# Gate and up projections of two SwiGLU layers by seven block products instead of eight, with the gated products spilled to DRAM and the down projection as a phase of its own

## The chip, the core and the metric

The kernel runs on one core of a Trainium2 chip. The metric is the device time of one execution in microseconds, as the median of several runs. TensorE multiplies, VectorE and ScalarE evict its results from PSUM and do the elementwise work, GpSimd works from SBUF alone, and DMAs are issued from the queues of SyncE and ScalarE.

## The reference

Two residual layers over 1024 tokens of width 1024, all in float32. Each layer is a mixer followed by a SwiGLU feed-forward of width 2816, and each of the two halves is normalised and modulated first:

```python
h = rms_norm(x, norm_ffn_g[l]) * (1 + sc2) + sh2
x = x + g2 * swiglu(h, ffn_w_gate[l], ffn_w_up[l], ffn_w_down[l])

def swiglu(h, w_gate, w_up, w_down):
    return (jax.nn.silu(h @ w_gate) * (h @ w_up)) @ w_down
```

The six modulation vectors of a layer come from a product of the conditioning vector with `ada_w[l]` (1024 x 6144). The mixer of layer 0 is a gated convolution beside a retention, that of layer 1 is a stick-breaking attention. The change touches only the feed-forward and the work at its edges.

## The kernel before

Activations lie transposed: `xT` and the normalised input `h` are [128 features, 8 feature tiles, 1024 tokens], and each is worked on in two halves of 512 tokens, h = 0 and 1. Every float32 product is made of three fp32r products: both operands are split into a high part and the rest, and `three` issues high x high, high x low and low x high, each a matmul of 128 x 128 weights with 128 x 512 moving data. One projection of 128 outputs for one half is 8 feature tiles x 3 = 24 matmuls into one of the four PSUM banks of `psG`.

The program is a list of phases in a fixed order, and every engine's queue is written out by hand with semaphores. Around the change the phases are out0 (output projection of the mixer), norm1, ffn0, norm2, qkv0 in layer 0 and out1, norm3, ffn1 and the writing of the output in layer 1.

A feed-forward phase (`ffn0`, `ffn1`) is eleven turns. A turn takes 256 hidden features: four weight slabs (gate and up for two tiles of 128) and two slabs of the down weight. SyncE loads a slab (512 KB) into one of two raw buffers, and GpSimd splits it in four quarters into an 8 KB slot: four TENSOR_SCALAR for the high part, then four TENSOR_TENSOR for the rest. TensorE makes 8 gate and up projections (192 matmuls). ScalarE applies SiLU from PSUM, VectorE multiplies (`L1959`) and splits the product (`L1553`, `L1555`) into `hid`. Then TensorE makes the 16 down steps of the turn, 6 matmuls each, and VectorE adds every step to `xT` (`L1975`). Nothing of the hidden layer leaves the core.

Beside ffn0 the modulation of layer 1 is worked out: SyncE loads pieces of `ada_w` (`ada_raw`, two buffers, four pieces in a turn), VectorE accumulates them (`L1567`, two operations a piece), and one small group of matmuls per turn (`ada_group`) brings the sums into columns.

norm1 and norm3 follow an output projection: ScalarE squares `xT`, VectorE adds the squares, a matmul with ones takes the mean, ScalarE takes the root (Ln, Exp), VectorE refines it (`newton`, four operations), and then each tile is normalised (`L1629`), rounded by ScalarE (`norm_hi`) and its rest taken by VectorE (`L1620`). Half 0 is normalised beside the projection of half 1. Half 1 is normalised beside the first four projections of half 0 in the feed-forward, 96 matmuls.

## Time and profile before

| | us |
|---|---|
| median of 3 runs | 2635.77 |
| lowest and highest run | 2628.8 and 2636.09 |
| span of the profiled execution | 2618.4 |
| median less span | 17.4 |
| TensorE busy | 2532.1 (97%) |
| GpSimd busy | 976.8 (37%) |
| ffn0, first to last matmul of the down steps | 563.3 to 1249.9 |
| ffn1, the same | 1929.5 to 2607.5 |

No time of its own is listed for the profiled execution, only its span, from the first to the last instruction. What lies around the span is taken as median less span. A matmul's duration in the trace overlaps the next one, so the pace of TensorE is read from a stretch with a count of matmuls, not from the duration of one.

### The profile page before, as it was taken

What the parts mean: (1) busy time and instruction counts of PE and PEld (TensorE: products, weight loads), DVE (VectorE), ACT (ScalarE), POOL (GpSimd) and SP (SyncE); (2) the same over time, 40 slices, a digit from 0 to 9 for tenths busy, and PEclk for the clock granted to TensorE, in tenths of its full rate; (3) what the DMA queues carried; (4) which work ended last, traced back from release to release, by engine and by line L of the source; (5) the groups of instructions that cost most, each with busy time, mean ns of one, the idle gap of its engine ahead of it and who ended that gap; (6) DMA issues with size and microseconds to landing.
All of it is one profiled execution on the core that took longest, in us unless ns stands there. A gap on an engine that the chain in (4) does not pass through costs nothing.

```text
span 2618.4 us, 34125 instructions
## 1 busy us (share of the span) xinstructions
PE 2532.1 (97%) x11386; PEld 2077.7 (79%) x11386; DVE 1317.7 (50%) x2082; ACT 562.8 (21%) x1031; POOL 976.8 (37%) x1604
## 2 busy tenths in 40 slices
...
GB/s 277 174 129 97 137 125 276 50 81 81 80 80 80 80 80 80 80 72 49 89 21 45 33 33 32 45 57 140 49 49 48 48 48 48 48 48 48 48 32 65
DMA packets 220646, 208.31 MB, mean 80 GB/s; under 512 B 6122, under 2 KB 166020, under 8 KB 220420
## 3 DMA queue, kind: packets, MB, share of 16 engines
...
## 4 chain that ended last, share of the span: by engine, by line
PE 89%; DVE 6%; issue 2%; ACT 2%; DMA 1%; ACTq 0%; POOL 0%; DVEq 0%; SPq 0%; POOLq 0%
PE psG L632 27%; PE psG L638 26%; PE psG L637 26%; PE psM L983 1%; PE psG L1024 1%; PE psO L632 1%; PE psZ L1013 1%; PE psO L637 1%; PE psO L638 1%; DVE n_t L1629 1%; DVE h_lo L1620 1%; PE psZ L632 1%; PE psZ L638 1%; PE psZ L637 1%; PE psM L683 0%
## 5 line engine op out<-in xcount | busy, mean ns | idle before, releaser
L632 PE MATMUL psG<-h_hi,w_split 128*128 128x512 f32 x2496 | 990.7, 397 | 26.1 <-DVE h_lo L1555 13.4
L637 PE MATMUL psG<-h_lo,w_split 128*128 128x512 f32 x2496 | 976.7, 391 | 0.0
L638 PE MATMUL psG<-h_hi,w_split 128*128 128x512 f32 x2496 | 976.4, 391 | 0.0
L611 POOL TENSOR_SCALAR w_split<-w_raw 128x256 fp32r<-128x256 f32 x800 | 362.5, 480 | 1566.6 <-PE psG L632 514.2
L615 POOL TENSOR_TENSOR w_split<-w_raw,w_split 128x256 fp32r<-128x256 f32 x800 | 622.8, 810 | 0.0
L632 PEld LDWEIGHTS psG<-h_hi,w_split 128*128 128x128 f32 x2496 | 471.6, 189 | 132.6 <-issue 19.8
L638 PEld LDWEIGHTS psG<-h_hi,w_split 128*128 128x128 f32 x2496 | 471.1, 189 | 100.8
L637 PEld LDWEIGHTS psG<-h_lo,w_split 128*128 128x128 f32 x2496 | 471.9, 189 | 98.7 <-issue 4.1
L1959 DVE TENSOR_TENSOR hid<-sil,psG 128x512 f32<-128x512 f32 x88 | 60.6, 688 | 721.2 <-PE psG L638 718.6
L1975 DVE SCALAR_TENSOR_TENSOR xT<-psG,mod,xT 128x512 f32<-128x512 f32 x352 | 259.6, 748 | 168.5 <-PE psG L638 168.3
L1125 ACT ACTIVATE sil<-psG 128x512 f32<-128x512 f32 x88 | 52.5, 599 | 1293.4 <-PE psG L638 1293.3
L632 PE MATMUL psG<-hid_hi,w_split 128*128 128x512 f32 x704 | 274.8, 390 | 0.8 <-DVE xT L1975 0.8
L638 PE MATMUL psG<-hid_hi,w_split 128*128 128x512 f32 x704 | 274.0, 389 | 0.0
L637 PE MATMUL psG<-hid_lo,w_split 128*128 128x512 f32 x704 | 273.9, 389 | 0.0
L632 PEld LDWEIGHTS psG<-hid_hi,w_split 128*128 128x128 f32 x704 | 132.1, 188 | 29.7 <-issue 2.3
L638 PEld LDWEIGHTS psG<-hid_hi,w_split 128*128 128x128 f32 x704 | 132.1, 188 | 27.6
L637 PEld LDWEIGHTS psG<-hid_lo,w_split 128*128 128x128 f32 x704 | 132.2, 188 | 27.1
L1567 DVE SCALAR_TENSOR_TENSOR ada_acc<-ada_raw,c_act,ada_acc 128x512 f32<-128x512 f32 x140 | 115.6, 825 | 7.5 <-DMA ada_raw<-in_ada_w 4.5
L1125 ACT ACTIVATE s_z<-s_z 128x128 f32<-128x128 f32 (+2 forms) x192 | 100.9, 525 | 6.1
L1555 DVE TENSOR_TENSOR hid_lo<-hid,hid_hi 128x512 fp32r<-128x512 f32 x88 | 69.3, 788 | 3.0
L1555 DVE TENSOR_TENSOR s_w<-s_w,s_w 128x128 fp32r<-128x128 f32 (+2 forms) x96 | 63.9, 665 | 3.3
L1125 ACT ACTIVATE n_sq<-xT 128x512 f32<-128x512 f32 x48 | 30.0, 630 | 140.3 <-DVE n_sum L1597 56.3
...
## 6 DMA issues: line engine op xcount, KB each, us to landing
ada_raw<-in_ada_w SPq DMA_DIRECT2D x80, 512.0 KB, 4.1
w_raw<-in_ffn_w_gate SPq DMA_DIRECT2D x44, 512.0 KB, 3.9
w_raw<-in_ffn_w_up SPq DMA_DIRECT2D x44, 512.0 KB, 3.8
w_raw<-in_ffn_w_down SPq DMA_DIRECT2D x44, 512.0 KB, 3.7
w_raw<-in_ev_w_in SPq DMA_DIRECT2D x28, 512.0 KB, 4.6
w_raw<-in_od_w_qkv SPq DMA_DIRECT2D x24, 512.0 KB, 3.9
...
x_spill<-xT ACTq DMA_DIRECT2D x2, 4096.0 KB, 12.6
```

The source lines that it names most:

```text
L611: nc.gpsimd.tensor_scalar(slot[:, 0, part], raw[:, part], 1.0, 1.0, ALU.mult, ALU.mult).then_inc(hi_done, 1)
L615: lo = nc.gpsimd.tensor_tensor(slot[:, 1, part], raw[:, part], slot[:, 0, part].bitcast(F32), ALU.subtract)
L632: mm = nc.tensor.matmul(o, st[0], mv[0], start=first, stop=False, **kw)
L637: nc.tensor.matmul(o, st[0], mv[1], start=False, stop=False, **kw)
L638: return nc.tensor.matmul(o, st[1], mv[0], start=False, stop=end, **kw)
L983: misc(phase, i, 2 * off + e, [lambda: nc.tensor.matmul(psM[:], ones_head, s_sq[:], start=True, stop=True)])
L1013: mm = nc.tensor.matmul(zbank[t % ZRING][:, c0:], split_c[:, 1], s_s[:, t % SRING, n, c0:], start=False, stop=n == 1, skip_group_check=True)
L1125: return nc.scalar.activation(o, i_, f, **kw)
L1555: V.tensor_tensor(o[1], i_, o[0].bitcast(F32), ALU.subtract).then_inc(lo_sem, 1)
L1567: V.scalar_tensor_tensor(acc, src, cc, acc, ALU.mult, ALU.add).then_inc(ada_step, 1)
L1959: V.tensor_tensor(hid32[:], sil[f][:], psG[:, bank(phase, s)], ALU.mult).then_inc(bank_read[bank(phase, s)], 1)
L1975: V.scalar_tensor_tensor(xT[:, m, half(h)], psG[:, b], mod[:, l * MOD + 5 * KT + m:l * MOD + 5 * KT + m + 1], xT[:, m, half(h)], ALU.mult, ...
```

## The change

For each pair i of 128-feature tiles (256 hidden features, as a turn before) the product of a weight matrix (gate or up) with the input is cut in 2 x 2 blocks: two hidden tiles by two halves of the feature dimension (k 0 to 3 and 4 to 7), and two halves of the tokens. It is made by seven block products (Winograd's form of Strassen's product) of 4 feature tiles x 3 = 12 matmuls, for gate (m = 0) and up (m = 1): 14 products, 168 matmuls.

- The sums of input blocks (`t1` to `t4`) are made once a layer, after the norm, by VectorE, rounded by ScalarE, and their rests are taken by VectorE or GpSimd (`t_sum`, `t_low`). The normalised tiles are written in place into `xT`, so `xT` is first written to DRAM by halves (`x_spill`, waited for through `fx_out`).
- The sums of weight blocks (`w_sum`, 8 a pair) are made by GpSimd for each pair, from raw slabs in four buffers `f_raw`. ScalarE makes the high part of a weight block (`w_high`), GpSimd its rest (`f_block`), into a ring of 8 blocks `f_w`. For the first 8 blocks of a layer GpSimd makes both.
- The four outputs are put together from PSUM and three stored sums by VectorE (`first_y`, `second_y`, `out_12`, `out_21`), then SiLU, product, rounding and rest, and the split product goes to DRAM (`f_spill`, 4 x 512 KB a pair).
- The down projection follows as a phase of its own (`ffb0`, `ffb1`), six turns over 1, 2, 2, 2, 2 and 2 pairs, 16 steps each: 6 matmuls a step in turn 0, 12 in the others. The split products are loaded back (`hid_load`, 2 MB a pair), for turn j + 1 as turn j begins. `x_old` is loaded from DRAM for turn 0.
- The 40 pieces of `ada_w` are loaded and accumulated in turns 1 to 4 of ffb0, and their loads are issued by ScalarE.
- The loops over turns are written out.

The layout of `h`, some slots and the order in which norm2's tiles are normalised change with it.

```diff
-CHUNKS = D_FF // P // 2
+PAIRS = D_FF // P // 2
...
+PRODUCTS = 14
+WRING = 8
+P_OF = ("11", "21", "t2", "t3", "t1", "22", "t4")
+SUMS = (("s1", 0), ("s3", 0), ("s1", 1), ("s3", 1), ("s2", 0), ("s2", 1), ("s4", 0), ("s4", 1))
+BLOCK_SUM = {4: 4, 5: 5, 6: 1, 7: 3, 8: 0, 9: 2, 10: 6, 11: 7}
...
+DOWN_TURNS = [(0,), (1, 2), (3, 4), (5, 6), (7, 8), (9, 10)]
+HID_OF = {0: 0, 1: 2, 2: 3, 3: 0, 4: 1, 5: 2, 6: 3, 7: 0, 8: 1, 9: 2, 10: 3}
...
+ADA_AT = [16 + 8 * k // 5 for k in range(40)]
+ADA_COLS_AT = [ADA_AT[4 * g + 3] + 1 for g in range(10)]
...
-    ("ffn0", CHUNKS, dict(slab=6, step=24, misc=1, ada=4)),
+    ("ffa0", 1, dict()),
+    ("ffb0", 1, dict(slab=22, step=96, misc=10, ada=40)),
...
+        f_raw = at("f_raw", WO, [4, D])
+        f_w = at("f_w", WO + 16 * KB, [WRING, 2, H], F32R)
+        f_tmp = at("f_tmp", RO, [2, H])
+        f_p1 = at("f_p1", RO + 4 * KB, [2, H])
...
+                if i == 0:
+                    out_freed(sp, l, r // 2)
+                else:
+                    sp.wait_ge(fw_ready, f_prod(l, i - 1, (11, 12, 13, 14)[r]))
...
+                i = PAIRS - 1
+                f_spill(l, i - 1, 3)
+                sp.wait_ge(fp_done, f_prod(l, i, 1) + 1)
+                hid_load(sp, l, 0)
+                f_spill(l, i, 0)
+                sp.wait_ge(fw_ready, f_prod(l, i, 9) + 1)
+                slab_load(f"ffb{l}", 0, 0)
+                sp.wait_ge(fp_done, f_prod(l, i, 7) + 1)
+                sp.wait_ge(fx_out, 32 * (l + 1))
+                sp.dma_start(x_old[:], x_dram.rearrange("k p t -> p k t")).then_inc(fx_back, 16)
+                sp.wait_ge(fp_done, f_prod(l, i, 9) + 1)
+                hid_load(sp, l, 1)
+                f_spill(l, i, 1)
+                sp.wait_ge(fp_done, f_prod(l, i, 11) + 1)
+                hid_load(sp, l, 2)
+                sp.wait_ge(fe_t12, 2 * f_turn(l, i) + 2)
+                slab_load(f"ffb{l}", 0, 1)
+                f_spill(l, i, 2)
+                f_spill(l, i, 3)
...
+                for i in range(1, PAIRS):
+                    for b in range(4):
+                        f_block(l, i, b)
+                    for n in range(6):
+                        w_sum(l, i, n)
+                    for b in range(4, 6):
+                        f_block(l, i, b)
+                    for n in range(6, 8):
+                        w_sum(l, i, n)
+                    for b in range(6, PRODUCTS):
+                        f_block(l, i, b)
...
+                for i in range(PAIRS):
+                    for p in range(PRODUCTS):
+                        m, name = p % 2, P_OF[p // 2]
+                        bank_free(i, p)
+                        pe.wait_ge(fw_ready, f_prod(l, i, p) + 1)
+                        o = banks[(0, 0, 2, 4, 2, 2, 4)[p // 2] + m]
+                        block = f_w[:, (PRODUCTS * i + p) % WRING]
+                        opens = p // 2 in (0, 2, 3)
+                        for k in range(4):
+                            if i == 0 and m == 0:
+                                operand_wait(name, k)
+                            mm = three(o, [block[:, q, P * k:P * k + P] for q in range(2)],
+                                       [q[:, k] for q in operands[name]], opens and k == 0, k == 3, skip_group_check=True)
+                        mm.then_inc(fp_done, 1)
...
+                for j, pairs in enumerate(DOWN_TURNS):
+                    for turn_pass in range(2):
+                        h = down_half(j, turn_pass)
                         for m in range(KT):
...
+                            s = 16 * j + 8 * turn_pass + m
+                            if (turn_pass, m) == (0, 0):
+                                for pair in pairs:
+                                    pe.wait_ge(fh_in[HID_OF[pair]], 32 * hid_count(l, pair))
+                            if s >= 4:
+                                pe.wait_ge(bank_read[bank(phase, s)], uses(phase, 0, s))
+                            for x, pair in enumerate(pairs):
+                                slab = DOWN_SLABS.index((pair, m // 4))
+                                if turn_pass == 0 and m % 4 == 0:
+                                    pe.wait_ge(slab_ready, C.at("slab", phase, 0, slab)[1] + 1 + RAW)
+                                wk = [slot_w(SLOT(phase, slab))[:, q].rearrange("p (k c) -> p k c", k=2) for q in range(2)]
+                                cs = slice(P * (m % 4), P * (m % 4) + P)
+                                for f in range(2):
+                                    mm = three(psG[:, bank(phase, s)], [q[:, f, cs] for q in wk],
+                                               [q[:, f, half(h)] for q in hidb[HID_OF[pair]]], x == f == 0, x == len(pairs) - 1 and f == 1)
+                            mm.then_inc(gemm_done, 1)
...
+                phase = f"ffb{l}"
+                act.wait_ge(fp_done, f_prod(l, PAIRS, 0))
+                for j in range(len(DOWN_TURNS)):
+                    if j + 1 < len(DOWN_TURNS) and j:
+                        act.wait_ge(gemm_done, G(phase, 0, 16 * j - 1))
+                        for pair in DOWN_TURNS[j + 1]:
+                            hid_load(l, pair)
+                    if l == 0 and 1 <= j <= 4:
+                        for k in range(10 * j - 10, 10 * j):
+                            ada_load(k)
...
+                for k in range(4):
+                    norm.h_tile(1, k)
+                    norm.h_tile(1, 4 + k)
+                    t_sum("t1", k)
+                    t_sum("t2", k)
+                    if k:
+                        t_low("t2", k - 1)
+                t_low("t2", 3)
+                for k in range(4):
+                    t_sum("t3", k)
+                    if k:
+                        t_low("t3", k - 1)
+                t_low("t3", 3)
+                for m in range(2):
+                    first_y(l, 0, m)
+                for k in range(4):
+                    norm.low(1, 4 + k)
+                for k in range(4):
+                    t_sum("t4", k)
...
+                            V.scalar_tensor_tensor(x, psG[:, b], mod[:, g2:g2 + 1], x_old[:, m, half(h)] if j == 0 else x,
+                                                   ALU.mult, ALU.add).then_inc(bank_read[b], 1)
+                            if norm and s in ADA_COLS_AT:
+                                group = ADA_COLS_AT.index(s)
+                                ada_cols(phase, 0, group, ada_cols_of(phase, 0, group))
+                            if norm and s in ADA_AT:
+                                ada(phase, 0, ADA_AT.index(s))
...
```

On ScalarE's queue, at the end of the gate and up phase of layer 0 and on into ffb0, stands this in the changed kernel (`f_stg` is the staged split product, `hid00` to `hid11` the buffers of two pairs, `f_spill` the DRAM tensor):

```order
L1401 ACTIVATE f_stg_96<-f_hid_95 128x512
L1771 DMA hid00_97<-f_spill 128x2x1024
L1771 DMA hid01_98<-f_spill 128x2x1024
L1771 DMA hid10_99<-f_spill 128x2x1024
L1771 DMA hid11_100<-f_spill 128x2x1024
L1780 DMA ada_raw0_106<-in_ada_w 128x2x512
L1780 DMA ada_raw1_107<-in_ada_w 128x2x512
```

The same pieces of `ada_w` stood on SyncE's queue before, each behind one weight slab of the turn:

```order
L548 DMA w_raw0_63<-in_ffn_w_gate 128x8x128
L516 ISA
L523 ISA
L523 DMA ada_raw0_87<-in_ada_w 128x2x512
L545 REGISTER_ALU
L548 DMA w_raw1_64<-in_ffn_w_up 128x8x128
L516 ISA
L523 ISA
L523 DMA ada_raw1_88<-in_ada_w 128x2x512
```

The pieces have moved to another queue, and ten at a time stand behind four loads of 1 MB each. The second piece of work that moves is SyncE's end of the gate and up phase (after), with the down weight's second slab (`w_raw1`) behind `x_old` and two pairs of `hid`:

```order
L641 DMA w_raw0_63<-in_ffn_w_down 128x2x512
L665 DMA x_old_105<-x_spill 128x8x1024
L634 DMA hid20_101<-f_spill 128x2x1024
L634 DMA hid21_102<-f_spill 128x2x1024
L625 DMA f_spill<-f_stg_96 128x2x512
L634 DMA hid30_103<-f_spill 128x2x1024
L634 DMA hid31_104<-f_spill 128x2x1024
L641 DMA w_raw1_64<-in_ffn_w_down 128x2x512
```

Before, SyncE had only slabs there, and a down step never waited for anything but slabs and `hid` of its own turn.

VectorE's queue behind the root of norm1's half 1, of before:

```order
L1629 SCALAR_TENSOR_TENSOR n_t_80<-xT,modA,n_r 128x512
L1629 SCALAR_TENSOR_TENSOR n_t_81<-xT,modA,n_r 128x512
L1620 SCALAR_TENSOR_TENSOR h_lo<-n_t_80,mod,h_hi 128x512
L1629 SCALAR_TENSOR_TENSOR n_t_80<-xT,modA,n_r 128x512
L1620 SCALAR_TENSOR_TENSOR h_lo<-n_t_81,mod,h_hi 128x512
```

And of the changed kernel, where `f_t_92` is the sum t2 and `f_t_87` its rest, which the fifth product multiplies:

```order
L2027 SCALAR_TENSOR_TENSOR xT<-xT,modA,n_r 128x512 x2
L2364 TENSOR_TENSOR xT<-xT 128x512
L2367 SCALAR_TENSOR_TENSOR f_t_92<-xT,mod 128x512
L2379 TENSOR_TENSOR f_t_87<-f_t_92,f_t_86 128x512
L2027 SCALAR_TENSOR_TENSOR xT<-xT,modA,n_r 128x512 x2
```

For each operand tile of t2 VectorE now does five operations instead of two.

## Rows read from the trace of the kernel before

**Rows 1.** The page: span, and busy time of each engine.
```profile
span 2618.4 us, 34125 instructions
...
PE 2532.1 (97%) x11386; PEld 2077.7 (79%) x11386; DVE 1317.7 (50%) x2082; ACT 562.8 (21%) x1031; POOL 976.8 (37%) x1604
```

**Rows 2.** Windows: first ten turns of ffn1, then nine of ffn0; engines as the head names them.
```profile
core 0: us, PE busy (x) PEld busy (x) DVE busy (x) ACT busy (x) POOL busy (x), PEclk, DMA share, GB/s
1929.50:2582.30 652.80, 652.80 (x2881) 540.54 (x2880) 194.56 (x280) 23.97 (x40) 257.00 (x456) 1.00 0.15 45
563.30:1161.20 597.90, 597.14 (x2666) 494.20 (x2665) 240.59 (x333) 21.59 (x36) 261.14 (x438) 1.00 0.26 79
```

**Rows 3.** The page, costliest groups: GpSimd's subtraction of a weight split.
```profile
L615 POOL TENSOR_TENSOR w_split<-w_raw,w_split 128x256 fp32r<-128x256 f32 x800 | 622.8, 810 | 0.0
```

**Rows 4.** Timeline of GpSimd: one split beside busy VectorE, one alone.
```profile
513.74 4.70 POOL L615 TENSOR_TENSOR w_split<-w_raw,w_split 128x256 fp32r<-128x256 f32 x4
...
556.70 2.82 POOL L615 TENSOR_TENSOR w_split<-w_raw,w_split 128x256 fp32r<-128x256 f32 x4
```

**Rows 5.** Timeline of VectorE: out0's end, and half 1 of norm1.
```profile
514.32 1.22 DVE L1629 SCALAR_TENSOR_TENSOR n_t<-xT,modA,n_r 128x512 f32<-128x512 f32 x1
515.47 2.37 DVE L1620 SCALAR_TENSOR_TENSOR h_lo<-n_t,mod,h_hi 128x512 fp32r<-128x512 f32 x2
...
518.42 1.47 DVE L1597 TENSOR_TENSOR n_sum<-n_sum,n_sq 128x512 f32<-128x512 f32 x2
525.66 0.69 DVE L1604 SCALAR_TENSOR_TENSOR n_t<-psM,n_r 128x512 f32<-128x512 f32 x1 [5.77 <-ACT n_r L1125]
...
528.30 1.42 DVE L1629 SCALAR_TENSOR_TENSOR n_t<-xT,modA,n_r 128x512 f32<-128x512 f32 x2
...
538.55 1.63 DVE L1620 SCALAR_TENSOR_TENSOR h_lo<-n_t,mod,h_hi 128x512 fp32r<-128x512 f32 x2
```

**Rows 6.** Timeline of ScalarE: first step of the root of norm1's half 1.
```profile
524.37 0.60 ACT L1125 ACTIVATE n_r<-psM 128x512 f32<-128x512 f32 x1 [5.20 <-PE psM L692]
```

**Rows 7.** Groups by line and form: VectorE with PSUM, and with SBUF alone.
```profile
L1975 DVE SCALAR_TENSOR_TENSOR xT<-psG,mod,xT 128x512 f32<-128x512 f32 x352 | 259.6, 748 | 168.5 <-PE psG L638 168.3
L1567 DVE SCALAR_TENSOR_TENSOR ada_acc<-ada_raw,c_act,ada_acc 128x512 f32<-128x512 f32 x140 | 115.6, 825 | 7.5 <-DMA ada_raw<-in_ada_w 4.5
L1555 DVE TENSOR_TENSOR hid_lo<-hid,hid_hi 128x512 fp32r<-128x512 f32 x88 | 69.3, 788 | 3.0
```

**Rows 8.** DMA issued from 391 to 396 us: KB each, us to landing.
```profile
h_hi<-m_spill ACTq DMA_DIRECT2D x1, 1792.0 KB, 10.9
h_lo<-m_spill ACTq DMA_DIRECT2D x1, 1792.0 KB, 16.5
...
m_spill<-r_ol ACTq DMA_DIRECT2D x1, 256.0 KB, 14.1
```

**Rows 9.** The page, DMA issues over the whole span.
```profile
ada_raw<-in_ada_w SPq DMA_DIRECT2D x80, 512.0 KB, 4.1
...
w_raw<-in_ffn_w_down SPq DMA_DIRECT2D x44, 512.0 KB, 3.7
...
x_spill<-xT ACTq DMA_DIRECT2D x2, 4096.0 KB, 12.6
```

**Rows 10.** Windows: DMA at full load, last column GB/s.
```profile
395.00:400.00 5.00, 5.00 (x28) 4.32 (x26) 4.45 (x9) 1.23 (x2) 0.32 (x1) 1.00 1.01 381
```

**Rows 11.** Windows around two waits of TensorE before out1.
```profile
1775.00:1784.00 9.00, 1.50 (x4) 0.71 (x4) 2.06 (x3) 0.60 (x1) 4.57 (x8) 0.50 0.42 143
...
1795.50:1800.80 5.30, 5.30 (x13) 4.10 (x14) 5.08 (x10) 0.00 (x0) 0.00 (x0) 0.50 0.72 197
1800.80:1806.00 5.20, 5.20 (x24) 4.31 (x23) 1.12 (x2) 0.00 (x0) 0.00 (x0) 0.99 0.92 330
```

**Rows 12.** Window of norm2: the first projection of qkv0.
```profile
1250.00:1264.50 14.50, 10.09 (x27) 5.55 (x26) 13.80 (x21) 6.62 (x10) 0.00 (x0) 0.76 0.17 67
```

More of the change, by code:

```diff
@@ L48 @@
 RAW = 2
-SIL = 2
 RPAR = 3
@@ L65 @@
 STAT = 1
-FFN_STAT = 2
 NEWTON = 2
@@ L109 @@
     ("norm3", 1, dict(misc=2)),
-    ("ffn1", CHUNKS, dict(slab=6, step=24)),
+    ("ffa1", 1, dict()),
+    ("ffb1", 1, dict(slab=22, step=96)),
 ]
@@ L400, in build @@
         ev_in, ev_out, od_in, od_out = w["ev_w_in"][0], w["ev_w_out"][0], w["od_w_qkv"][0], w["od_w_out"][0]
+        DOWN_SLABS = [(pair, c) for turn in DOWN_TURNS for c in range(2) for pair in turn]
         def slab_src(phase, i, s):
@@ L435, in slab_ap @@
         def slab_ap(raw, phase, s):
-            n = 2 if phase in ("ffn0", "ffn1") and s >= 4 else KT
+            n = 2 if phase in ("ffb0", "ffb1") else KT
             return raw.rearrange("p (k c) -> p k c", k=n)
@@ L579, in _ @@
             for phase, iters, P_ in STREAM:
+                if phase in ("ffb0", "ffb1"):
+                    gate_up(int(phase[-1]))
                 def body(i):
@@ L963, in _ @@
             out_proj("out0", "norm1", 3)
-            ffn("ffn0", "norm1", "norm2")
+            gate_up(0)
+            down("ffb0", "norm2")
             def qkv_piece(phase, i, off, n):
@@ L1096, in _ @@
             out_proj("out1", "norm3")
-            ffn("ffn1", "norm3")
-            for last_step in range(20, 24):
-                bank_wait(pe, "ffn1", CHUNKS - 1, last_step)
+            gate_up(1)
+            down("ffb1")
+            for last_step in range(92, 96):
+                bank_wait(pe, "ffb1", 0, last_step)
             for t in range(4, KT):
@@ new lines, in hid_load, with ada_load @@
+            def hid_load(l, pair):
+                for n in range(2):
+                    act.wait_ge(fs_out[n], 32 * (f_turn(l, pair) + 1))
+                b = HID_OF[pair]
+                for q in range(2):
+                    act.dma_start(hidb[b][q][:].bitcast(F32), f_dram[2 * pair:2 * pair + 2, q].rearrange("f p t -> p f t")).then_inc(fh_in[b], 16)
+            def ada_load(k):
+                static, n = C.at("ada", "ffb0", 0, k)
+                act.wait_ge(ada_step, ADA_FREE + 2 * n - 2)
+                group, part = divmod(k, ADA_PIECES)
+                c = ada_cols_of("ffb0", 0, group) - MOD
+                rows = w["ada_w"][1][2 * P * part:2 * P * part + 2 * P, c * P:c * P + ADA_COLS]
+                act.dma_start(ada_raw[static % 2][:], rows.rearrange("(k p) c -> p k c", p=P)).then_inc(ada_in[static % 2], 16)
```

653 lines of the change are left out of this document (481 added, 172 removed), and 2 rows, old and new, of the table ADA_AFTER.

## The prediction

> **What bounds the kernel now.** I read the busy times first. TensorE is busy for 2532.1 of 2618.4 us, VectorE half of it, GpSimd 37% [rows 1]. Then the windows of the feed-forward: ten turns of ffn1 take 652.80 us for 2880 matmuls, so 65.28 us a turn and 0.2267 us a matmul, with TensorE busy throughout at full clock [rows 2]. Nine turns of ffn0 take 597.9 us, 66.4 a turn; the rest over ffn1 is the work on `ada_w`. So in the feed-forward only TensorE counts: a matmul less is 0.2267 us less, as long as no other engine or load comes to take its place. The reader should next look for what has slack there: GpSimd works 25.7 us a turn.
>
> **Matmuls removed.** Gate and up need 192 matmuls a turn, now 14 x 12 = 168. 24 x 22 pairs = 528 matmuls, x 0.2267 = **-119.7 us**. The down projection keeps its number (96 + 5 x 192 = 11 x 96), and its evictions fall from 176 to 96 a layer, which gains nothing, since they hide behind TensorE. The written-out loops cost nothing: turns in the loop and outside it run at the same pace.
>
> **GpSimd in steady state.** A pair is 28 TENSOR_TENSOR for the rests and 16 for the sums, 44 of 256 columns. Alone, four take 2.82 us, 0.70 each; beside VectorE's operations on SBUF, 4.70, 1.17 each [rows 4], and VectorE's slow from 0.71 to 1.2 likewise [rows 5]. Those with a PSUM operand stay at 0.748, those on SBUF alone average 0.79 to 0.83 [rows 7]. Of VectorE's 18 operations a pair 11 read PSUM and 7 do not (three `hidden`, four `hid_low`). Each of the 7 costs GpSimd about 0.45, so 44 x 0.70 + 7 x 0.45 = 34.0 us against 168 x 0.2267 = 38.1 for TensorE. With the page's mean of 0.81, collisions in it, it is 35.6 [rows 3]. The ring lets GpSimd run at most 8 blocks ahead: followed through a pair, its rest of block 3 is ready 2.1 us after TensorE ends product 9 of the pair before, six sums and block 4 take 12 more, and TensorE wants block 4 at 21.8. So no wait, **0**, with 7 us of slack. If it has none, it costs what the rivals say. ScalarE's 24 operations of 0.6 to 0.72 us are 16 of 38 us. Loads and spills are 4 MB a pair, 11 us at 381 GB/s [rows 10].
>
> The Trainium skill (SBUF — State Buffer, Who interferes with whom) has it that a VectorE instruction with two SBUF inputs and a GpSimd instruction exclude each other, one blocking fully. Taken so, each of the 7 blocks GpSimd for its whole 0.69 us: 30.8 + 4.8 = 35.6 us, still under 38.1. Row and rule give the same sum, but by the rule only 2.5 us of slack are left. In the trace four operations beside a busy VectorE took 4.70 us, not twice 2.82 [rows 4], so the rule is a little harder than the row; it is why the second rival has a chance at all.
>
> **Start of gate and up.** Let T be the end of the output projection (517.3 in layer 0). Before, 96 matmuls of half 0 (21.8 us) covered the norm of half 1, whose root began 7.1 us after T [rows 6] and whose last tile was ready at 540.2, T + 23 [rows 5]. Now only 48 (10.9 us, products 0 to 3) need nothing of half 1. The mean of half 1 follows product 0; root and refinement take 4 us, so it is there at T + 7.5. But the tiles are normalised in place and wait for the write of half 1's `xT`: 2 MB, half of the 4 MB that took 12.6 [rows 9], by a 2 us start about 7.5, from T + 1.6: T + 9.2. Then VectorE needs for each of four k two normalisations, two sums and a rest, 3.5 us alone, and about 4.3 while GpSimd takes the rests of t1 (the factor of [rows 4]): the rests of t2 end at T + 27, where the fifth product was due at 10.9. Product 5 runs at the low clock at first, t3 follows in time: product 7 ends at T + 38.2, where eight products take 21.8. That is 16.4. In this pair GpSimd also has the high parts and eight rests of inputs: 1.5 more. Before lost 1 to 2 here. **+16.5 a layer, +33**; bounds 11 (no collision) and 24 (all of them, and a late write).
>
> **Start of the down phase.** Let E be the end of the last product. SyncE issues `x_old` (4 MB) after product 7, at E - 16.3, a pair of `hid` (2 MB) at - 10.9, a spill, another pair at - 5.4, and only then slab 1, all on one queue. A queue lands in order: 256 KB issued 3.2 us behind `h_lo` landed 14.1 us later, together with it [rows 8]. At 400 GB/s, near [rows 10], the first four are through at E + 8, slab 1 lands at 10, and GpSimd needs 4.3 (1.5 and 2.82). TensorE wants it after four steps of 6 matmuls, at E + 5.4, and waits to 14.3. That is 9, and 2.5 for the clock (next): **+11.5 a layer, +23**; bounds 5 and 20.
>
> **The clock.** After a wait of 8 us and one of 6 us the granted clock stands at 0.50 (1.2 of 2.4 GHz), and 13 matmuls after the second take 5.3 us in place of 2.9 [rows 11]. I add 2.5 us for each long wait.
>
> **The pieces of `ada_w`.** When turn j (1 to 4) begins, ScalarE issues 4 MB of `hid` and behind it ten pieces. In order, the first lands after 1.5 + 10.4 + 1.3 and the landing, with slabs beside it: 15 us ([rows 8] and [rows 10] again; a piece alone takes 4.1 [rows 9]). VectorE wants it at 3.5 us, just behind the first step of the turn, and everything behind it waits, evictions too. In turns 2 and 4 the group of sums is due on TensorE after three steps (8.2 us) and needs two pieces, 15 + 2 x 1.65 + 0.5 = 18.8: 10.6 lost, 13 with the clock. In turns 1 and 3 TensorE runs five steps to 13.6, waits for a bank to 17.2, then for the fourth piece: 8.5, 10.5 with the clock. **+47**; bounds 20 (pieces not held up by `hid`'s whole length) and 60. Before had SyncE load them with nothing long ahead.
>
> **norm2.** The first projection of qkv0 and the mean took 14.5 us where 5.4 of matmuls stand, with the clock at 0.76 [rows 12]. Now VectorE normalises a tile a step through the last turn and is 8 to 9 us behind at its end: **-4**; bounds -8 and +4.
>
> **Sum.** -119.7 + 33 + 23 + 47 - 4 = -20.7 us. On the span: 2618.4 - 20.7 = 2597.7; with the 17.4 around it (median less span), **2615 us**.
>
> **Rivals.**
> - *The waits hide.* If pieces and slabs interleave with the bulk loads, the terms 47 and 23 shrink to their lower bounds, 20 and 10: 2635.8 - 119.7 + 33 + 10 + 20 - 4 = 2575. It speaks for it that two queues do share the DMA engines, against it that all these loads stand on one queue, and [rows 8]. Chance 0.17.
> - *GpSimd becomes the bound* and the kernel is slower. It decides when 44 operations and collisions pass 38.1 us, 0.87 each all in. At 0.95, nearer to the 1.17 of [rows 4] than I think likely, a pair is 41.8: 22 x 3.7 = +81, so 2696. Against: VectorE collides in 5 of 38 us. Chance 0.08.
> - *The waits reach their upper bounds*: 48 + 40 + 60 + 4 - 119.7 = +32, 2668. Slower. It takes bulk loads slower than the 381 GB/s of [rows 10], which 1.8 MB in 10.9 us (`h_hi`, [rows 8]) speaks for, and the low clock after each short wait too. Chance 0.13.
> - *A bare swap*: gain and waits cancel within 8 us. It is a part of the likeliest case's width. Chance 0.12.
>
> The forecast (2590 to 2627) has 0.50.
>
> **Numbers.** 0.3% is 8 us, about what a measurement of this kernel can tell from no change. Faster: 0.17 + 0.50 and little else, 0.67; same 0.12; slower 0.21. The range leaves out the far end of the last rivals and the best of the first: 2570 to 2650.
>
> **What would show it.** 10,858 matmuls in place of 11,386; pairs at 38.1 us with TensorE busy (right for GpSimd's slack; longer pairs, with TensorE waiting for `f_w`, for the rival). TensorE waiting for `f_t` some 16 us at the start of both layers, for a weight slab 9 us at the start of both down phases, and for `ada_acc` or a bank in ffb0 alone, four times, 8 to 11 us each, with VectorE waiting for `ada_raw` just before. ffb0 would be some 47 us longer than ffb1. The forecast is wrong if the pieces land within 5 us, if GpSimd's operations average over 0.87, or if x's write takes over 12 us.

## The result: 0.7% slower, and the profile after

The changed kernel takes 2646.55 us (median of 8, 2641.51 to 2649.89), the kernel before, run beside it, 2631.91 (2622.37 to 2639.08): ratio 1.0067, 95% interval 1.0047 to 1.0087. The forecast was 2615, with 0.67 for faster. The time lies in the range 2570 to 2650, the sign is wrong.

The profiled execution took 2648.86 us, its span is 2647.1. The page, as [rows 1]:

```profile
span 2647.1 us, 31990 instructions
...
PE 2458.8 (93%) x10858; PEld 2006.9 (76%) x10858; DVE 1422.1 (54%) x2094; ACT 818.3 (31%) x1479; POOL 1358.1 (51%) x1932
...
L726 POOL TENSOR_TENSOR f_w<-f_raw,f_w 128x256 fp32r<-128x256 f32 x528 | 416.4, 819 | 79.6 <-ACT f_w L1401 79.5
...
L2427 DVE TENSOR_TENSOR f_stg<-f_hid,f_stg 128x512 fp32r<-128x512 f32 x88 | 115.4, 1311 | 190.8 <-ACT f_stg L1401 188.8
...
hid<-f_spill ACTq DMA_DIRECT2D x32, 1024.0 KB, 10.6
```

The 528 matmuls are gone and TensorE is busy 73 us less, but the span is 28.7 us longer than that of [rows 1]. Windows show where; their columns are the stretch, its length, then busy time and count for each engine, the granted clock, DMA share and GB/s. First, in layer 0: pairs 0, 1 and 2 of gate and up, then turns 0 to 4 of the down phase. Then, in layer 1: pairs 0 and 1, turns 0 and 1.

```profile
520.90:584.20 63.30, 47.71 (x171) 36.13 (x172) 48.56 (x56) 24.89 (x40) 52.89 (x59) 0.84 0.23 75
584.20:629.50 45.30, 40.71 (x169) 33.20 (x168) 14.33 (x18) 14.41 (x26) 38.53 (x51) 0.92 0.29 94
629.50:667.70 38.20, 38.20 (x169) 31.49 (x169) 16.73 (x18) 13.84 (x26) 33.62 (x46) 1.00 0.34 111
973.20:1008.80 35.60, 24.82 (x98) 19.98 (x97) 12.97 (x18) 0.63 (x1) 23.68 (x46) 0.81 0.60 226
1008.80:1068.30 59.50, 51.24 (x210) 41.60 (x209) 26.63 (x38) 0.00 (x0) 16.28 (x27) 0.89 0.56 190
1068.30:1133.60 65.30, 49.57 (x218) 40.81 (x216) 27.85 (x40) 0.00 (x0) 19.89 (x32) 0.87 0.54 178
1133.60:1192.20 58.60, 50.42 (x210) 41.15 (x210) 26.07 (x38) 0.00 (x0) 18.75 (x32) 0.91 0.57 197
1192.20:1256.60 64.40, 49.45 (x218) 40.70 (x217) 27.82 (x40) 0.00 (x0) 19.88 (x32) 0.87 0.53 179
1928.00:1993.40 65.40, 48.39 (x171) 36.44 (x172) 48.18 (x56) 24.88 (x40) 53.56 (x60) 0.82 0.22 73
1993.40:2036.90 43.50, 40.00 (x170) 32.68 (x169) 14.33 (x18) 14.55 (x26) 37.52 (x51) 0.96 0.29 97
2380.60:2416.00 35.40, 24.16 (x97) 19.51 (x96) 12.96 (x19) 0.63 (x1) 23.15 (x45) 0.81 0.60 220
2416.00:2459.50 43.50, 43.50 (x193) 36.04 (x192) 12.00 (x16) 0.00 (x0) 15.26 (x28) 1.00 0.41 146
```

At 0.2267 us a matmul a pair is 38.1 us, turn 0 21.8 and a later turn 43.5. Steady pairs and turns 1 to 4 of layer 1 are there, TensorE busy throughout. The loss is in three places, for both layers together where it is in both: pairs 0 and 1 (108.6 and 108.9 for 76.2, so 65), turn 0 (13.8 and 13.6, so 27), turns 1 to 4 of layer 0 (247.8 for 174.1, so 74; some 11 of this the kernel before had too: 66.4 for 65.3 us a turn in ten turns, by [rows 2]).

What TensorE waits for, in layer 0: inside product 4 (the first with t2), before product 10, and in turn 0, there with GpSimd's row beside it:

```profile
544.25 0.80 PE L863 MATMUL psG<-f_t,f_w 128*128 128x512 f32 x1 [3.97 <-DVE f_t L2379]
...
571.56 0.50 PE L863 MATMUL psG<-h_hi,f_w 128*128 128x512 f32 x1 [3.78 <-DVE f_y L2433]
...
989.50 0.76 PE L863 MATMUL psG<-hid,w_split 128*128 128x512 f32 x1 [10.78 <-POOL w_split L846]
...
985.12 1.51 POOL L842 TENSOR_SCALAR w_split<-w_raw 128x256 fp32r<-128x256 f32 x4 [19.70 <-DMA w_raw<-in_ffn_w_down]
```

Turn 2 in the timeline, VectorE, then TensorE, then ScalarE's queue (start, length, what, and in brackets the idle time and what ended it):

```profile
1071.22 0.75 DVE L2487 SCALAR_TENSOR_TENSOR xT<-psG,mod,xT 128x512 f32<-128x512 f32 x1 [1.97 <-PE psG L869]
1088.29 1.54 DVE L1960 SCALAR_TENSOR_TENSOR ada_acc<-ada_raw,c_act,ada_acc 128x512 f32<-128x512 f32 x2 [16.32 <-DMA ada_raw<-in_ada_w]
...
1092.00 1.86 PE L914 MATMUL psM<-consts,ada_acc 128*128 128x1 f32 x8 [15.38 <-DVE ada_acc L1960]
...
1068.49 2.02 ACTq L1771 DMA_DIRECT2D hid<-f_spill  x4
1070.55 21.80 ACTq L1780 DMA_DIRECT2D ada_raw<-in_ada_w  x4
```

ScalarE issues 4 MB of `hid` at 1068.5, the piece of `ada_w` behind it at 1070.6, and VectorE has it at 1088.3. The loads of this queue land in the order of issue: the four of `hid` at 1075.7, 1079.5, 1083.3 and 1087.0, the piece at 1088.3. Windows, the middle of that load and the first 6 us behind the wait:

```profile
1072.00:1086.00 14.00, 4.62 (x21) 3.49 (x19) 0.00 (x0) 0.00 (x0) 5.41 (x10) 0.82 1.01 380
...
1092.00:1098.00 6.00, 6.00 (x18) 5.13 (x19) 0.76 (x2) 0.00 (x0) 0.00 (x0) 0.51 0.43 139
```

DMA runs full, at the 381 GB/s of [rows 10], and after the wait 18 matmuls take 6 us at half clock.

### The profile page after: what moved, and what is told of

It is laid out like the page before. It is cut to its first block, busy times and chain, and to the rows that moved or that the text cites. A ratio compares the mean times of both kernels' runs of the same rounds, so it can differ in the third digit from the quotient of the medians.

```text
span 2647.1 us, 31990 instructions
## 1 busy us (share of the span) xinstructions
PE 2458.8 (93%) x10858; PEld 2006.9 (76%) x10858; DVE 1422.1 (54%) x2094; ACT 818.3 (31%) x1479; POOL 1358.1 (51%) x1932
## 4 chain that ended last, share of the span: by engine, by line
PE 78%; DVE 10%; DMA 6%; POOL 2%; issue 2%; ACT 2%; ACTq 0%; SPq 0%; DVEq 0%; POOLq 0%
PE psG L863 20%; PE psG L868 20%; PE psG L869 20%; PE psZ L863 3%; PE psZ L869 3%; PE psZ L868 3%; DMA ada_raw<-in_ada_w 3%; DMA w_raw<-in_ffn_w_down 1%; DVE xT L2027 1%; PE psM L1258 1%; PE psG L1299 1%; DVE ada_acc L1960 1%; PE psZ L1288 1%; PE psO L863 1%; DVE h_lo L2014 1%
## 5 line engine op out<-in xcount | busy, mean ns | idle before, releaser
L863 PE MATMUL psG<-h_hi,w_split 128*128 128x512 f32 x1088 | 440.5, 405 | 22.0 <-DVE h_lo L1948 12.6
L726 POOL TENSOR_TENSOR f_w<-f_raw,f_w 128x256 fp32r<-128x256 f32 x528 | 416.4, 819 | 79.6 <-ACT f_w L1401 79.5
L868 PE MATMUL psG<-h_lo,w_split 128*128 128x512 f32 x1088 | 429.7, 395 | 0.0
L869 PE MATMUL psG<-h_hi,w_split 128*128 128x512 f32 x1088 | 429.3, 395 | 0.0
L846 POOL TENSOR_TENSOR w_split<-w_raw,w_split 128x256 fp32r<-128x256 f32 x448 | 357.1, 829 | 0.0
L863 PE MATMUL psG<-hid,w_split 128*128 128x512 f32 x704 | 284.0, 403 | 33.1 <-POOL w_split L846 22.0
L863 PE MATMUL psG<-h_hi,f_w 128*128 128x512 f32 x704 | 281.8, 400 | 16.2 <-ACT f_p L1401 8.1
L868 PE MATMUL psG<-hid,w_split 128*128 128x512 f32 x704 | 280.6, 399 | 0.0
L869 PE MATMUL psG<-hid,w_split 128*128 128x512 f32 x704 | 280.0, 398 | 0.0
L868 PE MATMUL psG<-h_lo,f_w 128*128 128x512 f32 x704 | 278.4, 395 | 0.0
L869 PE MATMUL psG<-h_hi,f_w 128*128 128x512 f32 x704 | 278.2, 395 | 0.0
L863 PEld LDWEIGHTS psG<-h_hi,w_split 128*128 128x128 f32 x1088 | 207.7, 191 | 70.4 <-issue 19.0
L869 PEld LDWEIGHTS psG<-h_hi,w_split 128*128 128x128 f32 x1088 | 207.4, 191 | 45.5
L868 PEld LDWEIGHTS psG<-h_lo,w_split 128*128 128x128 f32 x1088 | 208.1, 191 | 44.0 <-issue 3.4
L863 PEld LDWEIGHTS psG<-hid,w_split 128*128 128x128 f32 x704 | 136.7, 194 | 63.1 <-issue 23.0
L863 PEld LDWEIGHTS psG<-h_hi,f_w 128*128 128x128 f32 x704 | 134.9, 192 | 50.8 <-ACT f_p L1401 12.9
L1401 ACT ACTIVATE n_sq<-xT 128x512 f32<-128x512 f32 x48 | 29.8, 630 | 421.3 <-DVE xT L2487 283.1
L869 PEld LDWEIGHTS psG<-hid,w_split 128*128 128x128 f32 x704 | 136.3, 194 | 29.5
```

The source lines that it names most:

```text
L726: lo = nc.gpsimd.tensor_tensor(slot[:, 1, parts[q]], src[:, parts[q]], slot[:, 0, parts[q]].bitcast(F32), ALU.subtract)
L846: lo = nc.gpsimd.tensor_tensor(slot[:, 1, part], raw[:, part], slot[:, 0, part].bitcast(F32), ALU.subtract)
L863: mm = nc.tensor.matmul(o, st[0], mv[0], start=first, stop=False, **kw)
L868: nc.tensor.matmul(o, st[0], mv[1], start=False, stop=False, **kw)
L869: return nc.tensor.matmul(o, st[1], mv[0], start=False, stop=end, **kw)
L1401: return nc.scalar.activation(o, i_, f, **kw)
```

## Experiments

"Changed" is the changed kernel, 2646.55 us; ratios are to the kernel before. Times of pairs and turns are read from each run's trace, from the first matmul of one to that of the next. The "high" of an operand is its rounded part, the "rest" what is left of it, and a "copy" is `first_copy`, ScalarE's copy of product 0 or 1 out of PSUM, before which TensorE can't go on with product 2 or 3.

### Pieces of ada_w first

```
+ for k in range(40):
+     ada_load(k)
+     j, at = k // 10 + 1, k % 10
+     if at == 1: act.wait_ge(gemm_done, G(phase, 0, 16 * j - 1))
+     if 1 <= at <= 4: <one 1 MB half of a pair of hid for turn j + 1>
```

> The pieces of ada_w go ahead of the hid loads on ScalarE's queue: two pieces, then one 1 MB hid load behind each of the next four pieces. If the pieces are late because they stand behind 4 MB on one queue, turns 1 to 4 of ffb0 (59.6, 65.2, 58.7 and 64.3 us in the changed kernel) fall to 44.5 to 46 each, TensorE's waits for ada_acc vanish, and the kernel is 64 to 68 us faster than the changed one: about 2580, 0.980 of the kernel before. If the cause is that the transfers as a whole fill the DMA engines, or that VectorE's work on the pieces itself is the delay, order changes little: 0 to 30 us, 0.993 to 1.007.

2589.51 us, ratio 0.9866 (0.9833 to 0.9898). Turns 1 to 4 take 49.2, 47.0, 45.5 and 47.1, 59 us less in all (44.5 to 46 each was expected), and the kernel is 57 us below the changed one, where 64 to 68 were expected. Windows of turns 1 and 2:

```profile
1006.40:1055.60 49.20, 47.30 (x209) 38.93 (x208) 28.53 (x38) 0.00 (x0) 18.47 (x30) 0.97 0.65 224
1055.60:1102.60 47.00, 46.64 (x217) 38.45 (x215) 28.87 (x40) 0.00 (x0) 21.66 (x32) 1.00 0.72 246
```

The same bytes are moved, in turn 2 at 246 instead of 178 GB/s, and TensorE hardly waits there. So it is the order on the queue, not the traffic as a whole. The edit does two things at once, which no run separates: it puts the pieces ahead, and it draws the four 1 MB loads of a turn apart (in turn 1 they are issued from 1006.6 to 1020.2, where the changed kernel issues turn 2's within 1.5 us). This edit alone makes the kernel faster than the one before. The Trainium skill (DMA: Bandwidth & Descriptors, Queues, rings and completion order) says that a DMA engine takes the descriptors of one ring in order. The trace agrees: the piece landed 1.3 us behind the last of the four loads ahead of it (1088.3 and 1087.0).

### Slab 1 ahead of the third pair of hid

```
- hid_load(sp, l, 2)
  sp.wait_ge(fe_t12, 2 * f_turn(l, i) + 2)
  slab_load(f"ffb{l}", 0, 1)
+ hid_load(sp, l, 2)
```

> Weight slab 1 of the down phase is issued ahead of the third pair of hid. If the wait in turn 0 (11.2 and 11.6 us) is the 2 MB ahead of it on the queue, slab 1 lands 5 us earlier and the wait falls by 5 to 8 us, with the slow clock behind it 7 to 10 a layer: 14 to 20 us in all, about 0.1 to 0.3% below the kernel before. If GpSimd's splitting of slab 1 is what ends it, or x_old alone holds it, the wait keeps over 8 us and the kernel gains under 8 in all.

2634.98 us, ratio 1.0027 (1.0011 to 1.0043). Turn 0 falls from 35.6 and 35.4 to 29.2 and 29.8, TensorE's wait in it from 11.2 and 11.6 to 6.2 and 6.4: 12 us in all, just under the 14 to 20 expected. The mechanism holds.

### The order in pair 0 on VectorE and ScalarE

VectorE takes `second_y(0, 0)` and `second_y(0, 1)` ahead of `hidden(0, 0)` and `hid_low(0, 0)`; ScalarE takes `silu(0, 0)` ahead of the highs of t4, and `first_copy(1, 0)` and `first_copy(1, 1)` two blocks earlier.

> In the first pair VectorE forms the second sums ahead of the first gated product, ScalarE takes silu before the highs of t4, and the two copies of pair 1 go ahead of weight highs that wait for GpSimd's sums. If the two stalls of 4.2 to 5.3 us (product 10 of pair 0, product 2 of pair 1) are only the order on VectorE and ScalarE, both go, and pairs 0 and 1 together lose 24 us a layer in place of 32.5: 16 us in all, ratio 1.001. If GpSimd is behind by then, the waits come back as waits for f_w: under 6 us in all.

2637.97 us, ratio 1.0034 (1.0013 to 1.0055). The stall before product 10 is gone (pair 0 from 63.3 to 58.9 in layer 0, from 65.4 to 60.0 in layer 1), but pair 1 rises to 46.2 and 45.5: 3.5 us a layer in all, where 8 were expected. ScalarE waits there for a sum of GpSimd's, in its timeline:

```profile
584.52 0.63 ACT L1401 ACTIVATE f_w<-f_raw 128x512 fp32r<-128x512 f32 x1 [16.12 <-POOL f_raw L753]
...
586.62 0.57 ACT L1401 ACTIVATE f_p<-psG 128x512 f32<-128x512 f32 x1
```

The second row is `first_copy`, for which TensorE waits. Neither of the two expectations was right as put. The copies stood two blocks earlier, but still behind a high that waits for a sum, and TensorE waited for the copy and not for `f_w`.

### Rests of t1 late on GpSimd

```
- pool.wait_ge(ft_hi, 16 * l + 2 * k + 1)
+ pool.wait_ge(ft_hi, 16 * l + 8)
```

and blocks 6 and 7 ahead of these rests.

> GpSimd takes the rests of t1 only when ScalarE has all the highs of t1 and t2. If the 4.9 us that VectorE needs for each of the four k is made of 3.5 of its own and of collisions with GpSimd, a k falls to about 3.7, TensorE's waits within product 4 from 4.0 to 2.8 each, and pair 0 loses 4 to 5 us less in each layer: 8 to 10 in all. If the pace is set by the hand-over between ScalarE and VectorE, or by single instructions of VectorE whatever GpSimd does, nothing changes (within 2 us).

2644.65 us, ratio 1.0056 (1.0024 to 1.0089). Product 4, where TensorE waits for t2 k by k, takes 9.51 instead of 12.43 us: 2.9 less, where three waits 1.2 shorter each would give 3.6. So GpSimd's rests do slow VectorE there. But the stall before product 10 grows by 1.4, and pairs 0 and 1 together win only 0.4 and 0.8, where 4 to 5 a layer were expected. A gain in front of a later wait.

### How much slack has GpSimd?

`w_sum` repeats the additions of s1 into unused space in pairs 1 to 10, four (then eight) more operations a pair.

> The changed kernel with four more additions of 256 columns a pair on GpSimd (pairs 1 to 10, into unused space). GpSimd is busy 33.6 of 38.2 us a pair; if what is left is real slack, 33.6 + 2.8 = 36.4 still fits: pairs stay at 38.17 us and the span at 2647 within 5 us. If GpSimd's waits inside a pair (6.5 us of the copies of the block it waits for) are part of a chain that TensorE also hangs on, a pair becomes 39.5 to 41 and the span 25 to 55 us longer.

> Eight more additions a pair: 33.6 + 5.6 to 6.8 = 39.2 to 40.4 us, over TensorE's 38.1. If GpSimd bounds once its sum passes TensorE's, pairs take 39.3 to 40.5 us and the span grows by 20 pairs x 1.1 to 2.3 = 22 to 46 us. If GpSimd's work is somehow hidden beyond that (its busy time overstated), pairs stay at 38.2.

Spans 2704.1 and 2792.2 us. Steady pairs take 40.97 with four more and 45.0 to 46.7 with eight, where 39.3 to 40.5 were expected. The four, 2.8 us of work, cost 2.8 us a pair, although GpSimd is idle for 4.6 us of each pair: its waits are part of a chain that TensorE hangs on too. What stands in between is seen in the changed kernel's steady state, ScalarE's timeline:

```profile
781.57 0.63 ACT L1401 ACTIVATE f_w<-f_raw 128x512 fp32r<-128x512 f32 x1 [9.31 <-POOL f_raw L753]
782.11 0.61 ACT L1401 ACTIVATE f_stg<-f_hid 128x512 fp32r<-128x512 f32 x1
...
786.49 0.61 ACT L1401 ACTIVATE f_w<-f_raw 128x512 fp32r<-128x512 f32 x1
787.01 0.58 ACT L1401 ACTIVATE f_p<-psG 128x512 f32<-128x512 f32 x1
```

ScalarE waits 9.3 us for GpSimd's fifth sum, to form the high part of block 4 of the next pair; then it works off what has gathered behind, and the copy of product 0 comes at 787.0, just when TensorE needs it for product 2. So the copy hangs on the sum only by ScalarE's order. The highs of blocks 4 to 7, which are made of sums, were then held back behind the copy of product 0:

```
  if p == 2: silu(i, 0)
+ if p == 0:
+     for late in range(loc - 4, loc): w_high(late + WRING)
- w_high(loc + WRING)
+ if p < 10: w_high(loc + WRING)
```

> The four extra additions again (40.97 us a pair, 2704), with one change of ScalarE's order in every pair: the highs of the blocks made of GpSimd's sums stand behind the copy of the next pair's first product. If the missing slack was ScalarE waiting in order for GpSimd's sum with the copy that TensorE needs behind it, pairs return to 38.1 to 38.4 us and the span to about 2647 to 2652. If GpSimd's own work and its ring bound the pair, it stays at 40.9.

> Eight extra additions with the same order (45.5 us a pair without it). GpSimd's sum is 33.6 + 5.6 to 6.8 = 39.2 to 40.4 us and now bounds by itself: pairs of 39.3 to 40.9 us, span 2670 to 2705. If the order is not the cause, 45.5 stays.

With the highs of blocks 4 to 8 behind both copies (`p == 1`, `loc - 5`), with four more additions and with none:

> Four extra additions a pair, and the highs of the blocks made of sums now behind both copies of the next pair. With the highs behind the first copy only, a pair took 38.61 us, 40.97 without. If ScalarE's order was all, pairs are at 38.1 to 38.2. If GpSimd's work is already the bound with 48 operations, 38.6 stays or grows.

> The changed kernel with that order alone. Pairs 2 to 10 from 38.17 to 38.08, 1.8 us in both layers together; pair 1 from 45.4 and 43.5 to 41 to 43, since the copy no longer stands behind a sum that comes late: 2 to 4 a layer. In all 6 to 10 us less than the changed kernel, 1.002 of the kernel before. If pair 1's wait is GpSimd's lateness itself, it comes back as a wait for block 4: 2 us in all.

One steady pair in each of five runs, from windows. Four more additions, the order as in the changed kernel:

```profile
799.70:840.70 41.00, 38.41 (x170) 31.47 (x169) 16.66 (x18) 13.82 (x24) 36.35 (x50) 1.00 0.32 103
```

Eight more, the same order:

```profile
771.60:816.60 45.00, 39.70 (x170) 32.43 (x169) 14.32 (x18) 13.79 (x24) 39.45 (x53) 0.96 0.28 94
```

Four more, highs behind the first copy:

```profile
821.10:859.70 38.60, 38.37 (x170) 31.45 (x169) 19.45 (x18) 14.07 (x24) 36.41 (x49) 1.00 0.33 109
```

Four more, highs behind both copies:

```profile
812.00:850.10 38.10, 38.10 (x169) 31.48 (x168) 21.90 (x18) 13.81 (x24) 36.44 (x49) 1.00 0.34 112
```

None more, highs behind both copies:

```profile
772.60:810.70 38.10, 38.10 (x169) 31.53 (x168) 19.78 (x18) 13.73 (x24) 33.32 (x45) 1.00 0.34 112
```

GpSimd's 36.4 us fit into 38.1 once ScalarE's order lets them. With eight more, held behind one copy, pairs 2 to 10 took 41.4 to 46.8 (expected 39.3 to 40.9), span 2750.4 (expected at most 2705): GpSimd's 39.4 us now exceed TensorE's 38.1, and the rest above that was not taken apart. The order alone gave 2638.83 us, ratio 1.0007 (0.9972 to 1.0043), and pair 1 at 38.08 us in both layers, from 45.4 and 43.5: the whole loss of pair 1 was this order, and the rival (a wait for block 4) did not come. But turn 0 rose from 35.6 and 35.4 to 38.8 and 40.2, which takes 8 of these 13 us back, and the median is 8 us below the changed kernel's. VectorE, then GpSimd, in a steady pair of that run:

```profile
789.76 7.02 DVE L2431 TENSOR_TENSOR f_stg<-f_hid,f_stg 128x512 fp32r<-128x512 f32 x1
...
787.82 2.84 POOL L726 TENSOR_TENSOR f_w<-f_tmp,f_w 128x256 fp32r<-128x256 f32 x4
790.61 5.62 POOL L726 TENSOR_TENSOR f_w<-f_raw,f_w 128x256 fp32r<-128x256 f32 x8
796.40 1.67 POOL L726 TENSOR_TENSOR f_w<-f_raw,f_w 128x256 fp32r<-128x256 f32 x2 [0.17 <-ACT f_w L1401]
```

VectorE's rest of the first gated product lasts 7.0 us, until GpSimd pauses. The same operation takes 0.69 at its shortest, and 3.0 at this place in the changed kernel, there too until GpSimd pauses. In the last pair the spill waits for that rest, and behind the spill SyncE holds slab 0 and `x_old`: `x_old` is issued 12.9 us before turn 0, in the changed kernel 16.1.

### A single input on GpSimd

```
- nc.gpsimd.tensor_tensor(slot[:, 1, part], src, slot[:, 0, part], ALU.subtract)
+ nc.gpsimd.tensor_scalar(slot[:, 1, part], src, 1.0, 1.0, ALU.mult, ALU.mult)
```

> The changed kernel with the highs behind both copies and the blocks' rests on GpSimd written by a TENSOR_SCALAR with one SBUF input instead of a subtraction with two (the rests are then not subtracted, so that part of the computation is left out; the number of operations is the same). VectorE's four rests of the gated products took 2.42 us each on average, up to 7.0, against 0.69 alone. If two-input operations of GpSimd keep VectorE's two-input operations out, the mean falls below 1.0 us in the stretches with rests alone, since only the sums (16 of 44) still collide. If any GpSimd work on SBUF does it, the mean stays above 1.8.

Span 2616.9 us. VectorE's rests average 0.82 us (from 2.42), `x_old` is issued 16.1 us before turn 0 again, and turn 0 falls from 38.8 and 40.2 to 35.1 and 34.4, which ties its growth to the long rest. But what was asked, whether two-input operations of GpSimd do it, is not settled: GpSimd's operations take 0.42 us now, and its stream was over when the rest came. Where one met it (785.11, GpSimd's own two operations took 1.16 instead of 0.78), it collided with one input too:

```profile
784.95 0.69 DVE L2431 TENSOR_TENSOR f_stg<-f_hid,f_stg 128x512 fp32r<-128x512 f32 x1
```
```profile
781.91 2.25 POOL L726 TENSOR_SCALAR f_w<-f_raw 128x256 fp32r<-128x256 f32 x6
785.11 1.16 POOL L726 TENSOR_SCALAR f_w<-f_raw 128x256 fp32r<-128x256 f32 x2 [0.95 <-ACT f_w L1401]
787.83 0.78 POOL L726 TENSOR_SCALAR f_w<-f_raw 128x256 fp32r<-128x256 f32 x2 [1.56 <-ACT f_w L1401]
```

### The edits together

First: pieces first, the order of pair 0, all highs of sums of pair 1 behind its two copies (pair 1 only), and on SyncE slab 1 ahead of two pairs of `hid`. Then the same with t1's rests late.

> Three edits at once, GpSimd's order untouched: ada_w's pieces first (as before: 59 us), slab 1 ahead of two pairs of hid (turn 0 from 35.5 to 22 to 24 us, 12 a layer), and in the first two pairs a further order on ScalarE, all its weight highs that wait for GpSimd's sums behind the copies of pair 1 (pairs 0 and 1 from 108.7 to 99 to 101 us, 8 to 9 a layer). About 2646.5 - 58 - 24 - 17 = 2548, 0.968 of the kernel before. If GpSimd is what is late in pair 1, pairs 0 and 1 stay at 104 to 105, and the kernel at 2556.

> The same with the rests of t1 late on GpSimd. Alone that edit took 2.9 us out of product 4 and gave it back at product 10, where VectorE came late. With VectorE's order changed too the 2.9 stay gone: 3 a layer less than the run beside it, about 2542. If GpSimd is the late one after product 4, the blocks behind the rests come later by as much, and the two runs are equal within 2 us.

2564.11 us, ratio 0.9734 (0.9694 to 0.9774), and 2564.28, 0.9736 (0.9697 to 0.9776), 16 and 22 above what was expected. Turn 0 at 23.3 and 23.8. Pairs 0 and 1 come to 102 and 103, with t1's rests late to 99 and 100, but pair 2 then takes 40.4 and 42.4, or 43.0 and 43.2: most of what pairs 0 and 1 gain by t1, pair 2 gives back. Turn 1 of layer 1 takes 51.5 in the first; slabs 2 and 3 stand behind `hid` there, and TensorE waits for GpSimd's splits twice, 1.5 and 3.0 us. Next, the highs held behind the first copy in every pair, and slab 2 ahead of the third pair of `hid`:

> The three edits of the run that gave 2564 us, with the highs held behind the first copy in every pair instead of once, and slab 2 ahead of the third pair of hid. The 0.1 us a pair and the 2.3 to 4.2 us that pair 2 lost go (5 to 8 in all), and turn 1 of both down phases falls by 4 to 7 us each (it stood at 49.3 and 51.5): about 2549, 0.967. If the waits move on again (GpSimd late in pair 1 whatever the order), 2558.

> The same with the rests of t1 late. Before, pairs 0 and 1 won 3 us a layer by it and pair 2 lost 3. If that loss was ScalarE's order, the 3 stay: 2543, 6 less than the run beside it. If GpSimd is late, they are equal within 2.

2560.09 us, 0.9744 (0.9718 to 0.9769), and 2559.43, 0.9739 (0.9712 to 0.9767), 11 to 16 above what was expected: steady pairs at 38.08 and turn 1 of layer 1 at 43.5, but pair 1 at 47.0 and 47.9, its second copy now behind the sums. Held behind both copies:

> The pieces first, slabs 1 and 2 ahead, VectorE's order of pair 0, and the highs behind both copies in every pair. Pair 1 from 47.0 and 47.9 to 42.8, pair 2 stays at 38.1: 9 us less than the 2560 of the run with the highs behind the first copy: about 2551, 0.970. If GpSimd is what is late, pair 1 keeps 45 and the kernel 2557.

> The same with the rests of t1 late: pair 0 down by 1.2 to 1.6 a layer and pair 1 by 1.6, the gain no longer taken back in pair 2: 2545, 6 less than the run beside it; equal within 2 if GpSimd is behind and takes it back.

2555.76 us, 0.9697 (0.9634 to 0.9760), and 2558.74, 0.9694 (0.9632 to 0.9757). Pair 1 at 41.3, turn 0 at 28.3 and 28.5. t1's rests late are worth next to nothing: product 4 wins 2.9 us, products 3, 6 and 9 lose 0.5 to 1.4 each, and pair 0 is left with 0.3 and 0.7. Turn 1 of layer 0 is back at 52.5 and 55.1, with TensorE waiting 4.1 and 5.8 us for `ada_acc`; why was not looked into. At last slab 0 and `x_old` ahead of the last pair's first spill:

> The run that gave 2556 us, with slab 0 and x_old issued ahead of the last pair's first spill. There that spill waited for VectorE's rest of the first gated product (7.0 us long, beside GpSimd's rests), and turn 0 took 28.3 and 28.5 us. If SyncE stood behind that spill, slab 1 lands some 4 us earlier and turn 0 falls to 23 to 25 us in both layers: 8 us in all, about 2548, 0.968. If the 6 MB themselves are what takes the time, turn 0 stays at 27 to 28.

2556.21 us, 0.9703 (0.9669 to 0.9736). `x_old` is issued 16.1 us before turn 0 instead of 12.9 and 12.6, and turn 0 still takes 28.3 and 28.1, as the rival had it: GpSimd waits for slab 1 to land,

```profile
963.30 2.33 POOL L843 TENSOR_SCALAR w_split<-w_raw 128x256 fp32r<-128x256 f32 x4 [13.98 <-DMA w_raw<-in_ffn_w_down]
```

14 us after the work before. In the first combination `x_old` was issued as early (16.1), and there GpSimd had slab 1 after 6.4 and 7.2 us, TensorE stood for 1.6 and 2.1 us and kept its clock; here it is 8.7 and 8.0 us, TensorE stands for 4.2 and 3.7 and loses it. The traces show most of the reason, and it is the edit's own doing: slab 0 and `x_old` were put ahead of the first spill, so that its 512 KB now stand between `x_old` and slab 1. That spill lands 2.7 and 3.5 us behind `x_old`, and slab 1 4.8 and 5.4 us behind it, 2.3 and 2.9 in the first combination. The last three versions are the fastest: 3% under the kernel before, 88 to 91 us under the changed one.

## Why the prediction was wrong

By its steps, in us for both layers:

| step | forecast | measured |
|---|---|---|
| 528 matmuls | -119.7 | -119.7 |
| GpSimd in steady state | 0 | +1.7 |
| start of gate and up | +33 | +60 |
| start of the down phase | +23 | +27 |
| pieces of ada_w in ffb0 | +47 | +63 |
| between the layers, norm2 with it | -4 | -6 |
| gate and up of layer 0 begin later | - | +3 |
| sum, on the span | -20.7 | +28.7 |

The first measured row is the count of matmuls at 0.2267 us; the rows add up to 29.0, and the 0.3 over the sum comes from rounding them. The row before the sum looks like scatter: in the runs above, with the same code up to that point, the first product begins between 517.1 and 521.1 us.

- **Matmuls removed: right.** 38.17 us a pair in steady state.
- **GpSimd in steady state: the number right, the reason wrong.** Its busy time is 33.6 us a pair, forecast 34.0. But the 7 us of slack weren't there: four more additions cost their full length. The forecast followed GpSimd from TensorE's ring to the blocks, and not on through ScalarE, whose queue had the high part of a sum ahead of the copy that TensorE waits for. The copy came 0.1 us late in each pair, and 5 to 7 us late in pair 1, where GpSimd is behind with pair 0's extra work. ScalarE waits 9.3 us for that sum in a steady pair and 14.9 in pair 1. Runs with the order changed show it: slack is back, pair 1 at 38.08.
- **Start of gate and up: the step that failed most**, +33 forecast, +60 measured (65, less 2 to 3 a layer that the kernel before lost there). Its first half was a matter of size: products 0 to 7 lose 19.5 and 20.6 us (forecast 16.4), since half 1's tiles start 11.7 us after the output projection (forecast 9.2) and each k of t2 takes 4.9 (4.3). The first of them in VectorE's timeline, with x's write just ahead:

```profile
531.94 1.41 DVE L2027 SCALAR_TENSOR_TENSOR xT<-xT,modA,n_r 128x512 f32<-128x512 f32 x2 [0.40 <-DMA x_spill<-xT]
```

  The write holds it up for 0.4 us here and 1.8 in layer 1, so the late write is not the cause. The second half was missing: the forecast followed the pair to product 7 only. Behind it come the stall of 4.2 before product 10, 5.7 and 6.7 us with the slow clock behind it (VectorE's second sums stand behind a gated product whose high ScalarE gives late; undone in the run with pair 0's order), and pair 1, 7.3 and 5.4, above. "1.5 more" for GpSimd's extra work stood in place of these 12 to 13 us a layer.
- **Start of the down phase: right**, 13.8 and 13.6 a layer for 11.5; TensorE's wait for slab 1 was 11.2 and 11.6 for 9. Slab 1 landed 11.8 and 12.3 us into the phase (forecast 10), 1.3 and 1.6 behind the last load ahead of it. Place and queue are shown by the run with slab 1 ahead. With slab 1 ahead of both pairs of `hid` the loss fell to 1.5 and 2; it rose to 6.5 again where VectorE's long rest comes in.
- **Pieces of ada_w: mechanism right, size too small.** It lost 16.1, 21.7, 15.2 and 20.8 in turns 1 to 4, forecast 10.5 and 13 alternately (before its 1.1 to 2 of own work). So the term that was mis-sized is the piece's landing. In turn 2 it comes 17.7 us after the issue and 20 into the turn, forecast 15: DMA ran at 380 GB/s as assumed, but 1.6 MB of slabs went beside the 4 MB of `hid`. Two pieces and an eviction later, 3.6 us, the group was there at 23.7, forecast 18.8. Even the upper bound of 60 was passed.
- **The clock: right.** 18 matmuls took 6 us behind the wait, 1.9 more than at full clock; turn 0 loses 2.0 to 2.6 beyond its wait.
- **Time around the span.** The forecast added median less span, 17.4. For the changed kernel the profiled execution's own time is 1.8 above its span: the 17.4 was mostly scatter of the kernel before, whose profile fell on one of its shorter executions. On spans the miss is 49 us, on medians 32.
- **Rivals.** The nearest was the waits at their upper bounds (48 + 40 + 60), given 0.13; in fact 60 + 27 + 63. GpSimd as the bound did not come by its own time, but the runs with extra additions show how near it was, by another way. "The waits hide" was refuted by the pieces.
